# Two of four weight sums of a block pair made by accumulating DMA transfers in a Strassen-type MLP product

## The chip, the cores and the metric

The kernel runs on one core of a Trainium2 chip. The metric is the device time of one launch in microseconds. Five engines work side by side, each in the order of its own program: TensorE (PE, with its weight loads as PEld), VectorE (DVE), ScalarE (ACT), GpSimd (POOL) and SyncE (SP, here only a queue of DMA issues). They meet through semaphores alone.

## The reference

```python
def reference(x, ...):                    # x (1, 512, 2048) float32, one layer
    u = rmsnorm(h, norm_mix); z = u @ w_in
    ...                                   # RWKV-7 heads and forgetting attention, side by side
    h = h + concatenate([y_rw, y_fox]) @ w_out
    u = rmsnorm(h, norm_mlp)
    h = h + square(relu(u @ w_ff1)) @ w_ff2        # w_ff1 (2048, 8192)
    gate = sigmoid(rmsnorm(h, norm_ple) @ w_ple_gate)
    h = h + gate * (p @ w_ple_proj)
    return rmsnorm(h, norm_final)
```

The change touches `u @ w_ff1` only: 512 tokens by 2048 by 8192, in float32 accuracy.

## The kernel before, in words

Float32 accuracy is had by splitting each operand into a high part (rounded to the multiplier's format, written by ACT) and a low part (operand less high part, written by DVE) and adding three products: high by high, high by low, low by high.

For `u @ w_ff1` the kernel uses a Winograd form of Strassen's method. The weights of 256 output columns make a pair (32 pairs, `PAIRS`): b11 and b12 are the first and second 128 columns of one half of the 2048 rows (128 partitions by 8 by 128 elements, 512 KB each), b21 and b22 the same of the other half. The activations are cut in the same way into A11, A12, A21, A22 with half of the tokens each. Instead of eight block products there are seven (`UNITS`, `seven_products`, L1188): the weight operands are b11, b21, b22 and four sums, bt1 = b12 - b11, bt2 = b22 - bt1, bt3 = b22 - b12, bt4 = b21 - bt2. The activation sums S1 to S4 are made once, while the output projection before still runs (`sum_tiles`, `mix_his`, `mix_los`). Each unit is eight times a 512-column and a 256-column matmul.

How one pair flows:

- SP loads the weights in two transfers of 1 MB: part 0 holds b11 and b12, part 1 b21 and b22 (L596). Part 0 of the next pair may be loaded once bt3 is made and b11 split; part 1 once bt4 is made and b22 split (L604 to L608).
- POOL makes bt1 to bt4 by `sum_weights` (L2708), in that order. bt1 needs part 0, bt2 part 1. Each waits until the buffer's last contents have been split.
- ACT writes the high part of each unit's weights (`product_hi`, L1686), DVE the low part (`product_lo`, L2323), into four slots. A slot is free when PE has done the unit that used it, about four units back.
- PE runs the units in the order of `LATER_PAIR`: b11, b21, bt2, bt1, bt3, b22, bt4. ACT and DVE split them in another order (`LATER_TURN`), here called turns: turn 0 is bt1, turn 1 b11, turn 2 b21, turn 3 bt2, turn 4 bt3, turn 5 b22, turn 6 bt4. So the first unit of a pair (b11) can only begin when bt1 and b11 have been split.
- Between the splits DVE adds up the products out of the PSUM banks (L2347 to L2395). Its order in the loop (L2436) is: split turn 0, `take_167` and `sum_22` of the pair before, split turn 1, `sum_12`, split turn 2, `sum_21`, split turn 3, then `begin_pair` with turns 4 to 6 and the reductions between them.
- After turn 3 ACT squares the pair's hidden values and stores them to DRAM (`store_hidden`).

Pair 0 is entered while the last tile of the output projection is still being turned into activation operands; pair 1 holds the root and the reciprocal of the norm. The SBUF of `parts` and `tsum` is that of the residual h, so the first loads wait until h has been stored to DRAM tile by tile (`h_stored_again`).

Of the kernel before, what the change touches and what calls it, by code (L numbers as in the profile page):

```python
# [56 lines left out]
         "mix_split": ("narrow_split", 1), "part_landed0": ("x_landed0", 64), "part_landed1": ("x_landed1", 64),  # L57
# [54 lines left out]
def build(nc, x, p, norm_mix, w_in, mu_shift, w0, w2, a0, a2, g2, k_k, k_a, r_k, gn_w, gn_b, b_f, q_norm,  # L112
# [270 lines left out]
    staged_all = sb("staged", [P, 6, 2, T], [base + 130 * 1024])  # L383
    staged = [staged_all[:, n, :, :] for n in (0, 1, 4, 5)]
# [3 lines left out]
    b11, b12, b21, b22 = parts[:, 0, :, 0:P], parts[:, 0, :, P:], parts[:, 1, :, 0:P], parts[:, 1, :, P:]  # L388
# [25 lines left out]
    free_after = (0, 1, 1, 2, 2, 3, 3, 4)  # L414
# [11 lines left out]
    with nc.Block() as block:  # L426
# [3 lines left out]
        def _(sp):  # L430
# [163 lines left out]
            def load_part(a, cols):  # L594

                sp.dma_start(parts[:, a, :, :], ff1_parts[:, a, :, cols]).then_inc(sg(f"part_landed{a}"), 16)  # L596
# [3 lines left out]
            for a in range(2):  # L600
                load_part(a, slice(0, 2 * P))
            with sp.Fori(0, PAIRS - 1) as i:
                for a in range(2):
                    sp.wait_ge(sg("weight_sums_made"), i * 4 + (past("weight_sums_made") + a + 3))  # L604
                    sp.sem_inc(sg("waits_taken"), 1)
                    sp.wait_ge(sg("w_split"), i * UNITS + (FIRST + 4 * a + 4))
                    sp.sem_inc(sg("waits_taken"), 1)
                    load_part(a, bass.ds(i * (2 * P) + 2 * P, 2 * P))  # L608

            def load_staged(q):  # L610

                if q < 4:
                    sp.wait_ge(sg("weight_sums_made"), past("weight_sums_made") + 4 * PAIRS)
# [65 lines left out]
        def _(pe):  # L679
# [504 lines left out]
            def mixed(u, j):  # L1184

                return mix_last[:, u, :] if j == NJ else mix[:, u, j, :]

            def seven_products(i, p):  # L1188

                for u, (_, x, dst, fresh) in enumerate(pair_order(p)):  # L1190
# [11 lines left out]
                    for j in range(UK):  # L1202
                        if p == 0 and u == 0 and j in (0, NJ):
                            pe.wait_ge(sg("mix_split"), past("mix_split") + (3 * NJ if j == 0 else 3 * NJ + 1))
                        if p == 0 and u in (2, 6) and j == NJ:
                            pe.wait_ge(sg("mix_split"), past("mix_split") + 3 * NJ + (2 if u == 2 else 3))
# [75 lines left out]
        def _(act):  # L1282
# [38 lines left out]
            def root(n):  # L1321
                act.wait_ge(sg("mean_square_ready"), n + 1)
                A(tmp[:, :], tmp[:, :], ACT.Sqrt).then_inc(sg("rms_ready"), 1)
# [319 lines left out]
            def scale_tile(i, f0, b):  # L1643
# [3 lines left out]
                act.wait_ge(sg("mix_split"), i * 3 + (past("mix_split") + 3 * (f0 // 2)))  # L1647
# [9 lines left out]
            def mix_his(i, j0, which):  # L1657
# [4 lines left out]
                if which == 0:  # L1662
                    act.wait_ge(sg("tile_scaled"), i * 2 + (past("tile_scaled") + 2 * j0 + 2))
                    A(to(0, 2), ev[:, :, 0:HT], ACT.Copy).then_inc(sg("mix_hi_ready"), 1)
                if which == 1:
                    act.wait_ge(sg("sums_made"), i * 4 + (past("sums_made") + 4 * j0 + 4))
                    A(to(2, 4), tile_sums[:, :, :], ACT.Copy).then_inc(sg("mix_hi_ready"), 1)
                if which == 2:
                    if j0 != NJ:
                        act.wait_ge(sg("h_stored_again"), i * 16 + past("h_stored_again"))  # L1670
                    A(to(6, 1), ev[:, 1:2, HT:T], ACT.Copy).then_inc(sg("mix_hi_ready"), 1)

            hi_unit(1, 0, M_OUT + KT // 2, a_turn=1)
            with act.Fori(0, NJ) as i:
# [5 lines left out]
                mix_his(i, 0, 0)  # L1680
                square_tile(i, 0, 1)
                mix_his(i, 0, 1)
                mix_his(i, 0, 2)


            def product_hi(i, p, u):  # L1686

                weights = pair_order(p)[u][0]
                for n, w in enumerate((b11, b21, b22)):
                    if weights is w:  # L1690
                        act.wait_ge(sg(f"part_landed{min(n, 1)}"), i * 16 + (past(f"part_landed{min(n, 1)}") + 16 * (p + 1)))
                for n, w in enumerate((bt1, bt2, bt3, bt4)):
                    if weights is w:
                        act.wait_ge(sg("weight_sums_made"), i * 4 + (past("weight_sums_made") + 4 * p + n + 1))
# [24 lines left out]
            mix_his(0, NJ, 0)  # L1719
            product_hi(0, 0, 2)  # L1720
            square_tile(0, 2 * NJ, 1)
            mix_his(0, NJ, 1)
            mix_his(0, NJ, 2)
            for u in range(3, UNITS):
                product_hi(0, 0, u)
# [93 lines left out]
        def _(dve):  # L1819
# [43 lines left out]
            def mean_square(n, sums=bank[3], rows=1):  # L1863
                dve.wait_ge(sg("sumsq_spread"), n + 1)
                V.tensor_scalar(tmp[:, :], sums[:, :], 1.0 / (rows * D), EPS, ALU.mult, ALU.add).then_inc(sg("mean_square_ready"), 1)

            def invert_root(n):

                dve.wait_ge(sg("rms_ready"), n + 1)
                then(V.reciprocal(rstd[:, :], tmp[:, :]))  # L1870
# [431 lines left out]
            def mix_los(i, j0, which):  # L2302

                def half(u0, n, c):
                    return mix_last[:, u0:u0 + n, c] if j0 == NJ else mix[:, u0:u0 + n, bass.ds(i, 1), c].rearrange("p u a t -> p (u a) t")

                u0, n, src = ((0, 2, ev[:, :, 0:HT]), (2, 4, tile_sums[:, :, :]), (6, 1, ev[:, 1:2, HT:T]))[which]
# [459 lines left out]
```

## Time and profile before

| | us |
|---|---|
| median of three runs | 2715.71 (2709.23 to 2717.53) |
| the profiled execution, its own time | 2714.75 |
| its span (first to last instruction) | 2713.2 |
| PE busy | 2587.8 (95% of the span) |
| DVE busy | 1608.7 (59%) |
| ACT busy | 1070.8 (39%) |
| POOL busy | 593.8 (22%) |
| stage of the 32 pairs, first to last matmul | 1096.1 to 1792.3 |

A busy PE in this profile is not a PE at its peak, since the ends of pipelined matmuls are modelled. Within the pair stage DVE is busy for over 80% of the time and POOL for about half. POOL's weight sums, 64 of the form `tsum<-parts` and 64 of the form `tsum<-parts,tsum`, take 367 us together.

### The profile page before, as it was taken

What the parts mean: (1) busy time and instruction counts of PE and PEld (TensorE: products, weight loads), DVE (VectorE), ACT (ScalarE), POOL (GpSimd) and SP (SyncE); (2) the same over time, 40 slices, a digit from 0 to 9 for tenths busy, and PEclk for the clock granted to TensorE, in tenths of its full rate; (3) what the DMA queues carried; (4) which work ended last, traced back from release to release, by engine and by line L of the source; (5) the groups of instructions that cost most, each with busy time, mean ns of one, the idle gap of its engine ahead of it and who ended that gap; (6) DMA issues with size and microseconds to landing.
All of it is one profiled execution on the core that took longest, in us unless ns stands there. A gap on an engine that the chain in (4) does not pass through costs nothing.

```text
span 2713.2 us, 48534 instructions
## 1 busy us (share of the span) xinstructions
PE 2587.8 (95%) x18322; PEld 2117.5 (78%) x18322; DVE 1608.7 (59%) x2001; ACT 1070.8 (39%) x1490; POOL 593.8 (22%) x389
## 2 busy tenths in 40 slices
PE   7999999999688999799999999999999999999998
PEld 5777777777577678687878878878888888888887
DVE  5566676666545555788878888863433343444444
ACT  4443444444456325344444444442222222233333
POOL 0000000000233006555555554510000000011110
PEclk9999999999899999899999999999999999999999
DMA  7555444555523335234434343474444444333333
GB/s 200 152 153 159 144 139 143 163 162 152 184 93 101 116 101 162 86 116 131 122 118 131 116 125 118 128 235 121 120 126 120 122 117 123 93 100 106 95 97 104
DMA packets 469437, 352.26 MB, mean 130 GB/s; under 512 B 56661, under 2 KB 435527, under 8 KB 468359
## 3 DMA queue, kind: packets, MB, share of 16 engines
q1 hardware_dynamic: 413111, 281.93, 36.1%
q0 software_dynamic: 11472, 39.43, 4.2%
q10 hardware_dynamic: 44800, 30.18, 3.3%
q8 instruction: 34, 0.56, 0.1%
q14 instruction: 20, 0.16, 0.0%
HBM read 294.21 MB, written 57.28 MB: 130 GB/s over the span
## 4 chain that ended last, share of the span: by engine, by line
PE 41%; issue 33%; DVE 9%; DMA 6%; POOL 5%; ACT 5%; SPq 1%; ACTq 0%; POOLq 0%; DVEq 0%
PE acc L698 7%; PE acc L700 7%; PE acc L699 7%; PE bank L1207 5%; DMA parts<-in_w_ff 4%; DVE w_lo L2328 4%; PE bank L1208 3%; POOL tsum L2723 2%; ACT w_hi L1699 1%; ACT w_hi L1304 1%; POOL sumsq L2559 1%; PE bank L886 1%; PE acc L896 1%; PE bank L896 1%; PE bank L906 1%
## 5 line engine op out<-in xcount | busy, mean ns | idle before, releaser
L1846 DVE TENSOR_TENSOR w_lo<-w_raw,w_hi 128x1024 fp32r<-128x1024 f32 x292 | 359.7, 1232 | 682.3 <-ACT w_hi L1304 674.9
L1207 PE MATMUL bank<-mix,w_hi 128*128 128x512 f32 x1561 | 575.4, 407 | 44.8 <-DVE w_lo L2328 31.4
L1304 ACT ACTIVATE w_hi<-w_raw 128x1024 fp32r<-128x1024 f32 x292 | 308.9, 1058 | 782.9 <-PE acc L700 725.7
L1208 PE MATMUL bank<-mix,w_lo 128*128 128x256 f32 x1561 | 442.7, 284 | 0.0
L698 PE MATMUL acc<-hidden,w_hi 128*128 128x512 f32 x1024 | 399.7, 390 | 3.1 <-DVE w_lo L1846 3.1
L1207 PEld LDWEIGHTS bank<-mix,w_hi 128*128 128x128 f32 x1561 | 299.6, 192 | 128.9 <-issue 38.8
L699 PE MATMUL acc<-hidden,w_hi 128*128 128x512 f32 x1024 | 399.4, 390 | 0.0
L700 PE MATMUL acc<-hidden,w_lo 128*128 128x512 f32 x1024 | 399.3, 390 | 0.0
L698 PE MATMUL acc<-a_all,w_hi 128*128 128x512 f32 x800 | 321.1, 401 | 2.1 <-DVE w_lo L1846 2.1
L700 PE MATMUL acc<-a_all,w_lo 128*128 128x512 f32 x800 | 312.9, 391 | 0.0
L699 PE MATMUL acc<-a_all,w_hi 128*128 128x512 f32 x800 | 312.4, 390 | 0.0
L1208 PEld LDWEIGHTS bank<-mix,w_lo 128*128 128x128 f32 x1561 | 301.3, 193 | 0.2 <-issue 0.2
L2328 DVE TENSOR_TENSOR w_lo<-tsum,w_hi 128x1024 fp32r<-128x1024 f32 x128 | 208.4, 1629 | 76.6 <-ACT w_hi L1699 75.9
L698 PEld LDWEIGHTS acc<-hidden,w_hi 128*128 128x128 f32 x1024 | 192.9, 188 | 43.6 <-issue 3.5
L2723 POOL TENSOR_TENSOR tsum<-parts,tsum 128x1024 f32<-128x1024 f32 x64 | 184.2, 2878 | 186.4 <-DMA parts<-in_w_ff 135.9
L700 PEld LDWEIGHTS acc<-hidden,w_lo 128*128 128x128 f32 x1024 | 192.8, 188 | 40.2
L699 PEld LDWEIGHTS acc<-hidden,w_hi 128*128 128x128 f32 x1024 | 192.9, 188 | 40.0
L2559 POOL TENSOR_TENSOR sumsq<-sumsq,sq 128x512 f32<-128x512 f32 x31 | 43.0, 1388 | 821.0 <-ACT sq L1319 821.0
L1699 ACT ACTIVATE w_hi<-tsum 128x1024 fp32r<-128x1024 f32 x128 | 135.7, 1061 | 210.7 <-PE bank L1208 134.9
L2723 POOL TENSOR_TENSOR tsum<-parts 128x1024 f32<-128x1024 f32 x64 | 183.0, 2859 | 123.5 <-DMA parts<-in_w_ff 117.4
L698 PEld LDWEIGHTS acc<-a_all,w_hi 128*128 128x128 f32 x800 | 150.6, 188 | 56.6 <-issue 22.0
L2328 DVE TENSOR_TENSOR w_lo<-parts,w_hi 128x1024 fp32r<-128x1024 f32 x96 | 190.9, 1988 | 6.2 <-ACT w_hi L1699 6.1
(364 smaller groups left out, 3905.3 us busy)
## 6 DMA issues: line engine op xcount, KB each, us to landing
parts<-in_w_ff SPq DMA_DIRECT2D x64, 1024.0 KB, 6.0
w_raw<-in_w_ff SPq DMA_DIRECT2D x128, 512.0 KB, 3.9
w_raw<-in_w_in SPq DMA_DIRECT2D x100, 512.0 KB, 3.9
w_raw<-in_w_out SPq DMA_DIRECT2D x32, 512.0 KB, 3.9
hid_d<-sq ACTq DMA_DIRECT2D x32, 512.0 KB, 5.7
w_raw<-in_w_ple_gate SPq DMA_DIRECT2D x32, 512.0 KB, 3.9
z_d<-ev POOLq DMA_DIRECT2D x50, 256.0 KB, 3.5
ev<-hid_d SPq DMA_DIRECT2D x24, 512.0 KB, 3.5
```

Of the source, the lines that this page charges most:

```text
L698: mm(dst, wh, hi[kt], start=kt == 0, stop=False)
L699: mm(dst, wh, lo[kt], start=False, stop=False)
L700: last = mm(dst, wl, hi[kt], start=False, stop=kt == KT - 1)
L896: last = mm(low(dst[g])[o, j, :], lhs(i, g * H + j), rhs(i, g * H + j), start=lv == 1 and j == 0, stop=lv > 1 or j == H - 1, skip_group_ch ...
L1207: mm(dst[:, :], wh[:, j, :], mixed(x, j), start=fresh and j == 0, stop=False, skip_group_check=True)
L1208: last = mm(dst[:, 0:HT], wl[:, j, :], mixed(x, j)[:, 0:HT], start=False, stop=j == NJ, skip_group_check=True)
L1304: A(w_hi[:, s, :, :], w_raw[:, s ^ raw_turned[0], :, :], ACT.Copy).then_inc(sg("w_hi_ready"), 1)
L1699: A(slots[slot_of[u]][0], weights, ACT.Copy).then_inc(sg("w_hi_ready"), 1)
L1846: V.tensor_tensor(w_lo[:, s, :, 0:width], w_raw[:, s ^ raw_turned[0], :, 0:width], w_hi[:, s, :, 0:width].bitcast(F32), ALU.subtract).then ...
L2328: V.tensor_tensor(lo, weights, hi.bitcast(F32), ALU.subtract).then_inc(sg("w_split"), 1)
L2559: G.tensor_tensor(sumsq[:, :], sumsq[:, :], sq[:, b, :], ALU.add).then_inc(sg("squares_summed"), 1)
L2723: G.tensor_tensor(dst, x, y, ALU.subtract).then_inc(sg("weight_sums_made"), 1)
```

## The change

Every weight sum becomes an addition: bt1 = b11 + b12, bt3 = b12 + b22, bt2 = bt1 + b22, bt4 = bt2 + b21. The signs go into the activation sums (s1 = a21 - a22, s4 = a12 + s2) and into two adds on the product side. bt1 and bt3 are no longer made by GpSimd instructions: SP loads one block straight into the sum's buffer and POOL issues a DMA that adds the other block to it in flight (`accum_op`). So SP issues five transfers of 512 KB a pair in place of two of 1 MB, POOL two accumulating ones of 512 KB and two sums in place of four. Blocks b12 and the second use of b22 are read from DRAM, not from `parts`. `LATER_PAIR`, `LATER_TURN` and the loop order on ACT and DVE stay as they are.

```diff
-    bt1, bt2, bt3, bt4 = (tsum[:, n, :, :] for n in range(4))
-    A11, A12, S2, S1, S3, S4, A22 = range(UNITS)
-    FIRST_PAIR = ((b11, A11, bank[0], True), (b21, A12, bank[1], True), (b22, S4, bank[2], True), (bt1, S1, bank[5], True),
+    bt1, bt3, bt2, bt4 = (tsum[:, n, :, :] for n in range(4))
+    A11, A12, S1, S2, S3, S4, A22 = range(UNITS)
+    FIRST_PAIR = ((b11, A11, bank[0], True), (b21, A12, bank[1], True), (bt1, S1, bank[5], True), (b22, S4, bank[2], True),
                   (bt2, S2, bank[0], False), (bt3, S3, acc[0], True), (bt4, A22, bank[4], True))
@@ SP
-            with sp.Fori(0, PAIRS - 1) as i:
-                for a in range(2):
-                    sp.wait_ge(sg("weight_sums_made"), i * 4 + (past("weight_sums_made") + a + 3))
-                    sp.wait_ge(sg("w_split"), i * UNITS + (FIRST + 4 * a + 4))
-                    load_part(a, bass.ds(i * (2 * P) + 2 * P, 2 * P))
+            def load_parts(p, i=0):
+                def room(sums_made, turn):
+                    if p:
+                        if sums_made:
+                            sp.wait_ge(sg("weight_sums_made"), i * 2 + (past("weight_sums_made") + 2 * (p - 1) + sums_made))
+                        sp.wait_ge(sg("w_split"), i * UNITS + (FIRST + UNITS * (p - 1) + turn + 3))
+                def load(dst, a, half, landed):
+                    sp.dma_start(dst, ff1_parts[:, a, :, bass.ds(i * (2 * P) + (2 * P * p + half * P), P)]).then_inc(sg(landed), 16)
+                room(1, 2 if p == 1 else 3)
+                load(bt1, 0, 0, "u_landed")
+                room(0, 1)
+                load(b11, 0, 0, "part_landed0")
+                ...
+                room(0, 5 if p == 1 else 4)
+                load(bt3, 0, 1, "v_landed")
+                if p:
+                    room(2, 2)
+                    load(b21, 1, 0, "part_landed1")
+                    room(1, 5)
+                    load(b22, 1, 1, "part_landed2")
+            load_parts(0)
+            sp.wait_ge(sg("h_ready"), 2 * KT)
+            sp.dma_start(h_v[:, KT - 2:KT, :], h[:, KT - 2:KT, :]).then_inc(sg("last_stored"), 16)
+            load_parts(1)
+            with sp.Fori(0, PAIRS - 2) as i:
+                load_parts(2, i)
@@ ACT, pair 0
+            product_hi(0, 0, 0)
             scale_tile(0, 2 * NJ, 0)
+            mix_his(0, NJ, "A11")
             square_tile(0, 2 * NJ, 0)
-            product_hi(0, 0, 0)
             product_hi(0, 0, 1)
...
@@ DVE, pair 0
+            product_lo(0, 0, 0)
             grow_tile(0, NJ, 0)
-            product_lo(0, 0, 0)
+            mix_los(0, NJ, "A11")
...
@@ POOL
+            def add_half(i, p, name, dst, a):
+                pool.wait_ge(sg(f"{name}_landed"), i * 16 + (past(f"{name}_landed") + 16 * (p + 1)))
+                pool.sem_inc(sg("waits_taken"), 1)
+                pool.dma_start(dst, ff1_parts[:, a, :, bass.ds(i * (2 * P) + (2 * P * p + P), P)], accum_op=ALU.add).then_inc(sg(f"{name}_summed"), 16)
+            def sum_weights(i, p, last):
+                if not last:
+                    pool.wait_ge(sg("u_summed"), i * 16 + (past("u_summed") + 16 * (p + 1)))
+                    pool.wait_ge(sg("part_landed2"), i * 16 + (past("part_landed2") + 16 * (p + 1)))
+                else:
+                    pool.wait_ge(sg("part_landed1"), i * 16 + (past("part_landed1") + 16 * (p + 1)))
+                    pool.wait_ge(sg("weight_sums_made"), i * 2 + (past("weight_sums_made") + 2 * p + 1))
+                if p:
+                    pool.wait_ge(sg("w_split"), i * UNITS + (FIRST + UNITS * (p - 1) + (6 if last else 4) + 3))
...
+                dst, x, y = (bt4, bt2, b21) if last else (bt2, bt1, b22)
+                G.tensor_tensor(dst, x, y, ALU.add).then_inc(sg("weight_sums_made"), 1)
             with pool.Fori(0, PAIRS - 1) as i:
-                for n in range(4):
-                    sum_weights(i, 1, n)
+                add_u(i, 1)                # add_half of "u" into bt1
+                add_v(i, 1)                # add_half of "v" into bt3
+                sum_weights(i, 1, False)
+                sum_weights(i, 1, True)
```

`product_hi` of bt1 waits for `u_summed`, of bt3 for `v_summed`. In pair 0 the last activation tile is mixed in five steps in place of three, with b11's split ahead of the tile's work; the last store of h moves from POOL to SP; the mean square of this norm is kept in `rstd` instead of `tmp`; and the buffers of the first staged hidden tiles move by one (`free_after` of tiles 3 and 4 goes from unit 2 to unit 3).

## Rows read from the trace of the kernel before

**Rows 1.** Busy time by stretch: us long, then each engine's, PEclk, DMA share, GB/s.
```profile
1096.00:1154.00 58.00, 45.31 (x216) 37.70 (x217) 48.57 (x43) 20.93 (x23) 32.84 (x16) 0.85 0.30 91
1154.00:1773.00 619.00, 589.83 (x3261) 504.90 (x3260) 519.49 (x526) 274.14 (x262) 332.48 (x117) 0.98 0.41 123
1773.00:1793.00 20.00, 20.00 (x115) 17.32 (x114) 17.72 (x21) 13.28 (x13) 5.76 (x2) 1.00 0.73 262
1850.00:2500.00 650.00, 650.00 (x2869) 538.25 (x2868) 261.88 (x277) 166.60 (x173) 22.13 (x15) 1.00 0.39 114
```
**Rows 2.** PE's waits, 1154 to 1773 us: total us, times, longest.
```profile
PE bank L1207 <- DVE w_lo L2328: 23.5, 22, 2.9
```
**Rows 3.** Timeline of ACT, an undisturbed pair: start us, us.
```profile
1425.82 1.06 ACT L1699 ACTIVATE w_hi<-tsum 128x1024 fp32r<-128x1024 f32 x1 [1.77 <-PE bank L1208]
...
1434.30 1.06 ACT L1699 ACTIVATE w_hi<-tsum 128x1024 fp32r<-128x1024 f32 x1 [1.77 <-PE bank L1208]
```
**Rows 4.** Timeline of POOL around a PE stall.
```profile
1400.22 3.41 POOL L2723 TENSOR_TENSOR tsum<-parts 128x1024 f32<-128x1024 f32 x1 [4.02 <-DMA parts<-in_w_ff]
1406.57 2.40 POOL L2723 TENSOR_TENSOR tsum<-parts,tsum 128x1024 f32<-128x1024 f32 x1 [2.94 <-DMA parts<-in_w_ff]
1408.93 2.55 POOL L2723 TENSOR_TENSOR tsum<-parts 128x1024 f32<-128x1024 f32 x1
1411.56 3.24 POOL L2723 TENSOR_TENSOR tsum<-parts,tsum 128x1024 f32<-128x1024 f32 x1
```
**Rows 5.** Timeline of all engines around the same stall.
```profile
1403.74 1.06 ACT L1699 ACTIVATE w_hi<-tsum 128x1024 fp32r<-128x1024 f32 x1 [3.63 <-POOL tsum L2723]
...
1404.83 1.23 DVE L2328 TENSOR_TENSOR w_lo<-tsum,w_hi 128x1024 fp32r<-128x1024 f32 x1 [2.26 <-ACT w_hi L1699]
...
1406.69 2.56 DVE L2381 TENSOR_TENSOR ev<-tile_sums 128x256 f32<-128x256 f32 x1
...
1409.17 3.39 DVE L2328 TENSOR_TENSOR w_lo<-parts,w_hi 128x1024 fp32r<-128x1024 f32 x1
...
1412.49 0.41 DVE L2386 TENSOR_TENSOR ev<-bank,tile_sums 128x256 f32<-128x256 f32 x1
...
1412.69 0.49 PE L1207 MATMUL bank<-mix,w_hi 128*128 128x512 f32 x1 [2.37 <-DVE w_lo L2328]
...
1413.27 2.61 DVE L2328 TENSOR_TENSOR w_lo<-parts,w_hi 128x1024 fp32r<-128x1024 f32 x1
...
1416.59 1.22 DVE L2328 TENSOR_TENSOR w_lo<-tsum,w_hi 128x1024 fp32r<-128x1024 f32 x1
```
**Rows 6.** SP's queue in 1410 to 1414 us.
```profile
1412.81 0.38 SPq L596 DMA_DIRECT2D parts<-in_w_ff  x1
```
**Rows 7.** DMA, 1154 to 1773: queue, packets, MB, share; issues, KB, us to landing.
```profile
q1 hardware_dynamic: 60320, 60.82, 35.1%
...
parts<-in_w_ff SPq DMA_DIRECT2D x58, 1024.0 KB, 6.1
```
**Rows 8.** DMA in 1850 to 2500 us, same columns.
```profile
q1 hardware_dynamic: 127174, 73.86, 39.2%
...
w_raw<-in_w_ff SPq DMA_DIRECT2D x116, 512.0 KB, 3.9
```
**Rows 9.** DMA of the whole span, transfers issued by POOL.
```profile
h_d<-h POOLq DMA_DIRECT2D x8, 512.0 KB, 3.2
...
h<-h_d POOLq DMA_DIRECT2D x2, 2048.0 KB, 10.7
```
**Rows 10.** Line L2740: duration ns min/median/max on POOL, first and last start.
```profile
L2740 POOL DMA_DIRECT2D h<-h_d x2: 889/903/917, 1793.1 to 1821.0; - x2
```
**Rows 11.** Timeline of DVE and PE where the pair stage begins.
```profile
1092.18 3.90 DVE L2328 TENSOR_TENSOR w_lo<-parts,w_hi 128x1024 fp32r<-128x1024 f32 x1 [2.31 <-ACT w_hi L1699]
...
1096.14 0.79 PE L1207 MATMUL bank<-mix,w_hi 128*128 128x512 f32 x1 [4.54 <-DVE w_lo L2328]
...
1140.09 0.77 PE L1207 MATMUL bank<-mix,w_hi 128*128 128x512 f32 x1 [7.79 <-DVE tile_sums L2347]
```

More of the change, by code:

```diff
@@ L1184, in mixed @@
             def mixed(u, j):
+                if j == NJ and u == A11:
+                    return row_hi[:, :]
                 return mix_last[:, u, :] if j == NJ else mix[:, u, j, :]
@@ L1322, in root @@
                 act.wait_ge(sg("mean_square_ready"), n + 1)
-                A(tmp[:, :], tmp[:, :], ACT.Sqrt).then_inc(sg("rms_ready"), 1)
+                mean = rstd if n == 1 else tmp
+                A(mean[:, :], mean[:, :], ACT.Sqrt).then_inc(sg("rms_ready"), 1)
             act.wait_ge(sg("gain_transposed"), 1)
@@ L1690, in product_hi @@
                     if weights is w:
-                        act.wait_ge(sg(f"part_landed{min(n, 1)}"), i * 16 + (past(f"part_landed{min(n, 1)}") + 16 * (p + 1)))
-                for n, w in enumerate((bt1, bt2, bt3, bt4)):
+                        act.wait_ge(sg(f"part_landed{n}"), i * 16 + (past(f"part_landed{n}") + 16 * (p + 1)))
+                for summed, w in (("u_summed", bt1), ("v_summed", bt3)):
                     if weights is w:
-                        act.wait_ge(sg("weight_sums_made"), i * 4 + (past("weight_sums_made") + 4 * p + n + 1))
+                        act.wait_ge(sg(summed), i * 16 + (past(summed) + 16 * (p + 1)))
+                for n, w in enumerate((bt2, bt4)):
+                    if weights is w:
+                        act.wait_ge(sg("weight_sums_made"), i * 2 + (past("weight_sums_made") + 2 * p + n + 1))
                 freed = FIRST + 2 + UNITS * p + (u - 2 if u < 3 else u - 6 if u == 3 else u - 3)
@@ L1864, in mean_square @@
                 dve.wait_ge(sg("sumsq_spread"), n + 1)
-                V.tensor_scalar(tmp[:, :], sums[:, :], 1.0 / (rows * D), EPS, ALU.mult, ALU.add).then_inc(sg("mean_square_ready"), 1)
+                V.tensor_scalar((rstd if n == 1 else tmp)[:, :], sums[:, :], 1.0 / (rows * D), EPS, ALU.mult, ALU.add).then_inc(sg("mean_square_ready"), 1)
             def invert_root(n):
                 dve.wait_ge(sg("rms_ready"), n + 1)
-                then(V.reciprocal(rstd[:, :], tmp[:, :]))
+                then(V.reciprocal(rstd[:, :], (rstd if n == 1 else tmp)[:, :]))
             def invert_rms(n):
@@ L2317, in _ @@
                 lo_unit(1, i * 2 + (OUT_U + 3))
-                mix_los(i, 0, 0)
-                mix_los(i, 0, 1)
-                mix_los(i, 0, 2)
+                for which in ("A1", "S1", "S", "A22"):
+                    mix_los(i, 0, which)
             def product_lo(i, p, u):
@@ L2418, in _ @@
             product_lo(0, 0, 4)
-            take_fifth(0, 0, 3)
+            take_fifth(0, 0, 2)
             product_lo(0, 0, 5)
@@ L2719, in sum_weights @@
                         pool.wait_ge(sg("w_split"), FIRST + 1)
-                if n in (1, 3):
-                    pool.wait_ge(sg("weight_sums_made"), i * 4 + (past("weight_sums_made") + 4 * p + n))
-                dst, x, y = ((bt1, b12, b11), (bt2, b22, bt1), (bt3, b22, b12), (bt4, b21, bt2))[n]
-                G.tensor_tensor(dst, x, y, ALU.subtract).then_inc(sg("weight_sums_made"), 1)
-            sum_weights(0, 0, 0)
+                dst, x, y = (bt4, bt2, b21) if last else (bt2, bt1, b22)
```

128 lines of the change are left out of this document (75 added, 53 removed).

## The prediction

> **What bounds the kernel now.** I read the busy times by stretch first. In the pair stage from 1154 to 1773 us PE is busy for 589.8 of 619 us, DVE for 519.5, POOL for 332.5, and the DMA engines for a share of 0.41 [rows 1]. The stretch holds 58 weight transfers, two a pair, so 29 pairs [rows 7] at 619 / 29 = 21.3 us each. Then the timeline of ACT in an undisturbed pair: its turns are released by PE, and from turn 0 at 1425.82 to turn 3 at 1434.30 three units pass, 2.83 us a unit [rows 3]. Seven units are 19.8 us. So a pair loses 1.5 us, 44 us over 29 pairs. PE's waits say where: 23.5 us of it PE waits for DVE's low parts, 22 times, at most 2.9 us [rows 2]; some 6 more in waits for DVE's sums, and the rest is the granted clock, 0.98 of 2.4 GHz on the mean, and 0.85 where the stage begins and the stalls are longer [rows 1].
>
> The rows around one stall show why DVE is late. bt1 was made by POOL from 1400.22 to 1403.63, because part 0 landed late [rows 4]. Only then could ACT begin turn 0, at 1403.74 [rows 5]. DVE follows, but POOL runs its other three sums, and an operation of DVE with two SBUF inputs does not run beside one: 2.56 us for a sum like the one that takes 0.41, 3.39 and 2.61 us for low parts that take 1.23 [rows 5], against POOL's own 2.4 [rows 4]. PE started at 1412.69, 9.1 us after bt1 was there. PE is the bound, with small stalls; nothing else is near it over the whole stage.
>
> **What it removes.** Two of POOL's four sums, so two locks on DVE a pair, and the chain over two pairs from part 1 by bt2, bt3, part 0 to bt1. If nothing took its place, all 44 us would go. At the stage's start, b11's split moves ahead of the tile's work and no weight sum runs beside it: it took 3.90 us in place of 1.23, and PE stood for 4.54 us [rows 11]. I count -5 us there (bounds 0 and -15: the later waits of pairs 0 and 1 need bt2 and the reciprocal as before, 7.79 us the longest [rows 11], and new transfers stand before them).
>
> **What it adds: a loop from pair to pair.** SP loads bt1's buffer for the next pair after turn 3 of this pair is split. In the loop turn 3 is DVE's last split before `begin_pair`, not its first. The new chain of one pair is: U (bt1 summed) - ACT and DVE, turns 0 to 3 - SP issues the load of b11 into bt1 - it lands - POOL issues the accumulating DMA - it lands, the next U. Nothing of PE is in it, so its sum is the shortest period of a pair.
>
> 1. U to the end of turn 3. In the stalled pair it took from 1403.74 to 1417.81, 14.1 us [rows 5]. The locks in it are 2.15, 2.16 and 1.38 us, 5.7 in all; without them 8.4. Afterwards POOL makes bt2 as soon as U is there, and bt4 right behind, as b21 and b22 have landed. bt2's 2.4 us [rows 4] run while ACT splits turn 0, and hold DVE's first low part for about 1.4 us; bt4's hold the next operation for about 2. So 11.8 us (bounds 8.4 and 14.1).
> 2. SP's issue: the last low part that it needed ended at 1412.56, it issued at 1412.81 [rows 5, 6]: 0.25.
> 3. The load of 512 KB in rows of 512 B: 3.9 [rows 8].
> 4. POOL's wait, registers, and start of the issue: 0.5. The chain before shows no such step; bounds 0.1 and 0.9, the latter the whole POOL time of an issue [rows 10].
> 5. The accumulating DMA from issue to landing. No row shows one. POOL's issue itself is 0.9 us for a transfer of as many rows [rows 10]. From below: 3.2, a plain store of 512 KB by POOL [rows 9]; a plain load of the same shape by SP is 3.9 [rows 8]. From above: 10.7, POOL's 2 MB in 1024 rows [rows 9], as if adding cost four times a copy. Two things add to 3.9. It must read its destination too: one more pass of 512 KB, 39.2% of 650 us for 73.86 MB [rows 8], which is 3.45 us a MB and 1.8 for 512 KB. And it shares the engines with what SP sends in the same microseconds (the loads of bt3's half, b21 and b22, 1.8 us each); I count one of the three as ahead of it, 1.8. I take 7.5.
>
> Sum: 11.8 + 0.25 + 3.9 + 0.5 + 7.5 = 23.95 us, over PE's 19.8 and over the 21.3 of now. Twenty-nine pairs times 2.65 = +77 us. The clock's falls cost nothing more then, since PE waits anyway.
>
> A page of the Trainium skill bears on step 5. Collectives: The Full Stack, "The bandwidth ceiling", states that an add in the DMA engines costs nothing itself but needs two source reads on one ring, and so runs at half the rate of a copy. No row of this case shows an accumulating transfer. By that rule the transfer would need 3.6 us of all engines in place of 1.8, which is what I added; by a rule that an add costs as a copy does, the loop would be 1.8 us shorter, 22.15 us, and the time about 2735.
>
> **The DMA engines.** Before, q1 takes 35.1% of 619 us for 29 pairs, 7.5 us a pair; with the hidden store, by the share of 0.41, 8.8 [rows 1, 7]. After: five loads of 1.8, the store 1.3, two accumulating transfers of 1.8 to 3.6: 14 to 17.6 us in a pair. That fits in 19.8, so it is no bound alone, and 0.73 was reached for 20 us [rows 1]; but transfers will meet each other far more often, which is the reason for taking more than 5.7 in step 5. If an add cost three passes it would be 21.1, the period of today.
>
> **The rest.** POOL: two issues of 0.9 and two sums of 2.4 in place of four sums, hidden, as POOL is busy for half the stage [rows 1]. Behind its wait for `u_landed` stands the DMA for bt3, and behind that the wait for `u_summed`, with bt2 and bt4; bt3 is wanted only in turn 4, after bt2, so that costs nothing. SP: its issues are in order, b21 waits for bt4 and b22 for turn 5, and all land before U. The turned signs change no duration. The end: hidden tile 3 waits for unit 3 instead of 2, 2.8 us later, but the tiles come in after the last sum of POOL and a DMA; 0, at most +3. The norm's root in `rstd`: 0.
>
> Total: 2714.8 + 77 - 5 = 2787 us by the profiled execution's own time, 1.6 above its span; it stands 1 below the median, so 2788.
>
> **The rivals.**
> A, faster: the loop closes within PE's 19.8 us. It does if steps 1 and 5 together are at most 15.2: for instance 10 us (DVE often takes its turn ahead of POOL's second sum, and turn 0 comes early enough that only turn 3 after PE counts) and 5.2 (an add is nearly a copy). For it: step 1 without locks is 8.4, a plain transfer is 3.9. Against it: both must be near their lower bounds at once. Then the 44 us of losses shrink to a few and the start gives 5: about 2673. It decides from a loop of 21.3 on, where steps 1 and 5 are 16.6.
> B, no change: the loop is 21.1 to 21.8 us, either by an add at the cost of a copy without crowding or by step 1 near 9.5. 2715.
> C, far slower: adding in flight costs more than two passes, or crowding takes three loads, so that step 5 is 10.7 or more. The loop is then 27.2 and more: 29 x 5.9 = +171, about 2880. Against it: nothing shows the engines near their limit now.
>
> **How the numbers follow.** Forecast 0.60, A 0.24, B 0.08, C 0.08. The forecast's own range, with step 1 from 11.5 to 12 and step 5 from 5.7 to 9.5, a loop of 21.9 to 26.2: 2730 to 2850. The range for 8 in 10 takes in most of A: 2668 to 2850. A measurement of this kernel tells 0.3%, 8 us, from no change. Faster 0.24; same 0.08; slower 0.68.
>
> **What would show it.** Right: PE waits for w_lo in almost every pair, 3 to 4 us each, at the first unit; the starts of the `hid_d` stores are 23 to 25 us apart; ACT's turn 0 is released by the DMA into tsum, not by PE; turn 3's low part, SP's load and POOL's issue follow each other without slack; the accumulating DMA lands 7 to 8 us after its issue. DVE's low parts have a lower mean than now, without PE gaining. Wrong: ACT's turn 0 still released by PE, or pairs 19.8 to 20.5 us apart (A), or the accumulating DMA landing within 5 us. At the start, b11's low part near 1.2 us and PE waiting under 1 us for it.

## The result, and the profile after

The changed kernel takes 2889.94 us (median of four runs, 2886.96 to 2890.87) against 2716.62 for the kernel before beside it: a ratio of 1.0643, with a 95% interval of 1.0624 to 1.0663. The forecast was 2788, with a range up to 2850. The sign and the mechanism were right, and the size was 2.4 times the forecast's: the profiled span grew from 2713.2 to 2888.7 us, by 175.5 where 72 had been summed. In this section and in the experiments two readings do most of the work: the distance of the `hid_d` stores, of which there is one a pair, so that their distance is the period of a pair, and the chain of waits through one pair.

First the busy times by stretch of the changed kernel, in the columns of [rows 1]:

```profile
1096.00:1154.00 58.00, 42.00 (x210) 35.10 (x210) 41.81 (x41) 22.04 (x26) 28.60 (x17) 0.88 0.80 164
1154.00:1900.00 746.00, 598.66 (x3062) 514.98 (x3063) 470.74 (x498) 255.50 (x247) 234.32 (x109) 0.87 0.71 153
```

PE was busy for 95% of the pair stage before and is busy for 80% of it now. Every engine is busy for a smaller share of it; only the DMA engines' share has risen, from 0.41 to 0.71. A stage in which no engine is the bound is bound by a chain of waits. The stores give its period; ahead of them the same row of the kernel before (duration min/median/max in ns, first and last start in us):

```profile
L1712 ACTq DMA_DIRECT2D hid_d<-sq x32: 338/338/353, 1134.4 to 1799.8; - x32
```

```profile
L1751 ACTq DMA_DIRECT2D hid_d<-sq x32: 338/338/353, 1131.4 to 1974.3; - x32
```

There are 31 steps between 32 stores. Before, a step was 665.4 / 31 = 21.46 us; after, 842.9 / 31 = 27.19. 31 x 5.73 = 177.5 us, less 3.0 because the first store comes earlier, plus 1.0 behind the last one: 175.5, the whole difference of the spans.

The waits of the changed kernel between 1200 and 1900 us (total us, times, longest), which answer to [rows 2]:

```profile
POOL tsum L2761 <- DMA tsum<-in_w_ff: 343.0, 50, 11.2
...
ACT w_hi L1738 <- DMA tsum<-in_w_ff: 162.4, 22, 8.1
...
PE bank L1234 <- DVE w_lo L2373: 138.3, 26, 6.1
```

PE waits for a low part once in each of the 26 pairs of this stretch, 5.3 us on the mean, where it was 22 short waits in the whole stage before. Behind it stands ACT's turn 0, which waits for the accumulating DMA into bt1. The chain of waits shows the loop itself. Here is one period, from the low part of turn 3 in one pair to that of the next (start us, us, what), with its small pieces left out:

```profile
1486.03 1.23 DVE w_lo L2373
...
1487.48 4.56 DMA tsum<-in_w_ff
...
1492.99 9.34 DMA tsum<-in_w_ff
...
1502.43 1.07 ACT w_hi L1738
...
1509.22 1.21 DVE w_lo L2373
...
1511.14 1.22 DVE w_lo L2373
...
1513.06 1.22 DVE w_lo L2373
...
1514.52 4.76 DMA tsum<-in_w_ff
...
1520.13 9.61 DMA tsum<-in_w_ff
...
1529.76 0.04 ACTq L1737
```

All five steps of the prediction's loop can be read off. Turn 3's low part ends at 1487.26; SP issues the load of b11 into bt1 at 1487.48; it lands 4.56 us later; POOL's issue of the accumulating DMA starts at 1492.99; it lands after 9.34 us; ACT begins turn 0 at 1502.43, and turn 3's low part ends at 1514.28, 27.02 us after the last one. There is no matmul in the chain.

What SP and POOL sent around that accumulating transfer, from the timelines of SP and then of POOL:

```profile
1514.52 0.37 SPq L606 DMA_DIRECT2D tsum<-in_w_ff  x1
1515.13 0.39 SPq L606 DMA_DIRECT2D parts<-in_w_ff  x1
1518.63 0.37 SPq L606 DMA_DIRECT2D tsum<-in_w_ff  x1
1519.47 2.82 SPq L606 DMA_DIRECT2D parts<-in_w_ff  x2
```

```profile
1520.13 1.56 POOL L2761 DMA_DIRECT2D tsum<-in_w_ff  x1 [11.12 <-DMA tsum<-in_w_ff]
1524.86 1.55 POOL L2761 DMA_DIRECT2D tsum<-in_w_ff  x1 [3.17 <-DMA tsum<-in_w_ff]
```

Three loads (bt3's half, b21, b22) leave within 3.7 us, around the accumulating DMA's issue at 1520.13; the load of b11, issued at 1515.13 and landed 7.0 us later, still runs for its first 2 us. bt3's own accumulating DMA follows at 1524.86; after it neither queue sends anything until the next turn 3. The DMA view of 1200 to 1900 us, in the columns of [rows 7]:

```profile
q1 hardware_dynamic: 132623, 66.87, 36.2%
q0 software_dynamic: 53719, 27.08, 30.7%
...
parts<-in_w_ff SPq DMA_DIRECT2D x76, 512.0 KB, 6.9
tsum<-in_w_ff SPq DMA_DIRECT2D x52, 512.0 KB, 5.0
tsum<-in_w_ff POOLq DMA_DIRECT2D x51, 512.0 KB, 9.0
```

q0 holds the 51 accumulating transfers: 0.307 x 700 / 51 = 4.2 us of all 16 engines each. q1 holds the 128 loads: 0.362 x 700 / 128 = 2.0 us each.

The median of 9.0 us mixes two kinds of transfer. Taken one by one between 1160 and 1950 us, the accumulating DMAs into bt1 land in 9.6 us (median of 29, 9.1 to 10.2) and those into bt3 in 8.5 (8.2 to 9.2). Only the first kind stands in the chain above, and it is the one compared in the experiments.

At the start of the stage, where [rows 11] had PE's first product of the pairs at 1096.14 after a wait of 4.54 us, the timelines of DVE and of PE now say:

```profile
1088.99 3.72 DVE L2373 TENSOR_TENSOR w_lo<-parts,w_hi 128x1024 fp32r<-128x1024 f32 x1
```

```profile
1092.77 0.50 PE L1234 MATMUL bank<-mix,w_hi 128*128 128x512 f32 x1 [1.08 <-DVE w_lo L2373]
```

b11's low part is still slow (3.72 us; POOL's sum of squares of the last tile runs beside it from 1089.65 to 1091.61), but it begins 3.2 us earlier, and the first product comes 3.4 us earlier.

### The profile page after: what moved, and what is told of

Same layout as the page of the kernel before. It is cut to its first block, busy times and chain, and to the rows that moved or that the text cites. A ratio compares the mean times of both kernels' runs of the same rounds, so it can differ in the third digit from the quotient of the medians.

```text
span 2888.7 us, 49206 instructions
## 1 busy us (share of the span) xinstructions
PE 2633.7 (91%) x18322; PEld 2158.6 (75%) x18322; DVE 1584.7 (55%) x2010; ACT 1067.8 (37%) x1499; POOL 502.6 (17%) x388
## 4 chain that ended last, share of the span: by engine, by line
PE 37%; issue 31%; DMA 16%; DVE 10%; ACT 4%; POOL 1%; SPq 1%; DVEq 0%; POOLq 0%; ACTq 0%
DMA tsum<-in_w_ff 14%; PE acc L723 7%; PE acc L725 7%; PE acc L724 7%; DVE w_lo L2373 4%; PE acc L1130 2%; PE acc L1132 2%; PE acc L1131 2%; PE bank L1234 1%; ACT w_hi L1738 1%; ACT w_hi L1331 1%; POOL sumsq L2606 1%; PE bank L911 1%; PE bank L921 1%; DVE tile_sums L2421 1%
## 5 line engine op out<-in xcount | busy, mean ns | idle before, releaser
L1234 PE MATMUL bank<-mix,w_hi 128*128 128x512 f32 x1561 | 618.4, 430 | 174.8 <-DVE w_lo L2373 166.8
L1234 PEld LDWEIGHTS bank<-mix,w_hi 128*128 128x128 f32 x1561 | 322.8, 207 | 263.0 <-issue 176.9
L1235 PE MATMUL bank<-mix,w_lo 128*128 128x256 f32 x1561 | 463.7, 297 | 0.0
L2373 DVE TENSOR_TENSOR w_lo<-tsum,w_hi 128x1024 fp32r<-128x1024 f32 x128 | 214.7, 1678 | 218.0 <-ACT w_hi L1738 218.0
L1235 PEld LDWEIGHTS bank<-mix,w_lo 128*128 128x128 f32 x1561 | 325.2, 208 | 0.2 <-issue 0.2
L2784 POOL TENSOR_TENSOR tsum<-tsum,parts 128x1024 f32<-128x1024 f32 x64 | 176.1, 2752 | 137.8 <-DMA parts<-in_w_ff 132.8
L2761 POOL DMA_DIRECT2D tsum<-in_w_ff x64 | 99.9, 1561 | 431.4 <-DMA tsum<-in_w_ff 417.5
L725 PEld LDWEIGHTS acc<-a_all,w_lo 128*128 128x128 f32 x800 | 150.5, 188 | 32.3
```

Of the source, the lines that this page charges most:

```text
L725: last = mm(dst, wl, hi[kt], start=False, stop=kt == KT - 1)
L1234: mm(dst[:, :], wh[:, j, :], mixed(x, j), start=fresh and j == 0, stop=False, skip_group_check=True)
L1235: last = mm(dst[:, 0:HT], wl[:, j, :], mixed(x, j)[:, 0:HT], start=False, stop=j == NJ, skip_group_check=True)
L2373: V.tensor_tensor(lo, weights, hi.bitcast(F32), ALU.subtract).then_inc(sg("w_split"), 1)
L2761: pool.dma_start(dst, ff1_parts[:, a, :, bass.ds(i * (2 * P) + (2 * P * p + P), P)], accum_op=ALU.add).then_inc(sg(f"{name}_summed"), 16)
L2784: G.tensor_tensor(dst, x, y, ALU.add).then_inc(sg("weight_sums_made"), 1)
```

## The experiments

Kernels are named by their labels. Those with an interval were timed in several rounds; the others are one run each. The kernel before stood beside them at 2709.46 (median) for e1 to e3 and e6, 2709.04 (one run) for e4, e5, e8 and e10, 2713.6 for e6b, e7 and e11, and 2716.35 for e12. The period is always (last store - first store) / 31 of the `hid_d` stores.

**e1_early_load: is it a loop, or the DMA engines?** The one wait that closes the loop is SP's, before it loads bt1's buffer. The buffer is free when turn 0 is split and bt2 is made; the changed kernel waits for turn 3.

```diff
-            def load_parts(p, i=0):
+            def load_parts(p, i=0, first=3):
-                room(1, 2 if p == 1 else 3)
+                room(1, 2 if p == 1 else first)
                 load(bt1, 0, 0, "u_landed")
-            with sp.Fori(0, PAIRS - 2) as i:
-                load_parts(2, i)
+            load_parts(2)
+            with sp.Fori(0, PAIRS - 3) as i:
+                load_parts(3, i, first=0)
```

> Changed kernel with one edit: from the fourth pair on SP may load bt1's buffer for the next pair once turn 0 (bt1) is split and bt2 is made, not only after turn 3. Theory 1, the loop from pair to pair (bt1 summed, turns 0 to 3, SP's load, POOL's accumulating DMA) sets the time: now 11.9 + 0.25 + 5.6 + 9.65 = 27.3 us; turn 0 ends 4.4 us after bt1 is summed, so the loop is 4.4 + 0.25 + 5.6 + 9.65 = 19.9 us, PE's own 19.8 is reached in places: 20 to 21 us a pair, total 2700 to 2725 us. Theory 2, the DMA engines are the bound (busy 0.71 of 27.1 us, 19.3 us a pair): the transfers crowd each other and land later the closer the pairs come, the period stays at 22 us or more, total 2750 us or more.

Measured: 2692.86 us (2689.41 to 2697.42), a ratio of 0.9937 (0.9919 to 0.9956) to the kernel before. One wait was worth 1.0643 - 0.9937 of the time before, 192 us, and what had lost 6.4% gains 0.6%. The time is 7 us under theory 1's range, with the period of 20.87 us inside the 20 to 21 that it gave, and far from theory 2's. Busy times and DMA view of 1200 to 1750 us in e1:

```profile
1200.00:1750.00 550.00, 535.30 (x3005) 460.40 (x3004) 441.18 (x484) 251.40 (x242) 230.56 (x108) 0.99 0.97 205
```

```profile
q0 software_dynamic: 55512, 27.99, 42.2%
...
parts<-in_w_ff SPq DMA_DIRECT2D x80, 512.0 KB, 7.8
tsum<-in_w_ff POOLq DMA_DIRECT2D x54, 512.0 KB, 7.0
```

The loop theory holds. The DMA engines are at a share of 0.97 here, and PE is busy for 97% of the stretch all the same. The accumulating transfers into bt1 land in 7.5 us (median; 6.8 to 9.4), sooner than the 9.6 of the changed kernel with its engines at 0.72, while SP's loads into `parts` land later than there (7.8 against 6.9). Within e1 the landing goes by what is issued next to it: 6.8 us where the next load of SP leaves 2.1 us behind the transfer, 9.4 where it leaves 0.8 us behind. So the mean load does not explain the 9.6; that the transfers of the same few microseconds do is what these readings and e3 below point to.

**e2_plain_copy: what does the adding cost?** The accumulating DMAs become plain ones.

```diff
-    ... (2 * P * p + P), P)], accum_op=ALU.add).then_inc(...)
+    ... (2 * P * p + P), P)]).then_inc(...)
```

> Changed kernel with the two DMAs of POOL as plain copies: the additions of bt1 and bt3 are left out. What the addition itself costs. If the second read is the cost (64.7 ns a packet against 30.9 for a plain one), POOL's transfer lands in 5.5 to 7 us in place of 9, the period is about 24 us and the total 2790 to 2810. If POOL's own way of issuing and the crowding by SP's loads are the cost, it still lands after 8.5 us or more, and the total stays above 2860.

Measured: 2830.58 us. Period 25.47 us, 1.7 less than in the changed kernel. Its DMA view of 1200 to 1750 us:

```profile
q0 software_dynamic: 6080, 22.15, 14.1%
...
tsum<-in_w_ff POOLq DMA_DIRECT2D x44, 512.0 KB, 6.9
```

Taken one by one, the plain copies land in 7.6 us into bt1 and 6.3 into bt3 (medians), where the accumulating ones took 9.6 and 8.5: in the same crowd the adding costs 2.0 to 2.2 us of landing, in which stands whatever its smaller packets cost (see the last section). By the periods the time fell by 31 x 1.72 = 53 us; it lies between the two expectations, nearer to the first. The adding is under a third of the loss of 178 us, not the whole of it.

**e3_thin and e4_thin_plain: the same without the crowd.** From pair 1 on every transfer of weights but the two into bt1 moves one eighth of its rows (bt3's DMA from POOL too, in the same way), so most of the weights stay those of pair 0; e4 also has plain copies, and leaves the two additions out as e2 does.

```diff
-    sp.dma_start(dst, ff1_parts[:, a, :, ...]).then_inc(sg(landed), 16)
+    n = 1 if p and landed != "u_landed" else UK
+    sp.dma_start(dst[:, 0:n, :], ff1_parts[:, a, 0:n, ...]).then_inc(sg(landed), 16)
```

> Changed kernel in which, from pair 1 on, all loads but that into bt1, and the accumulating DMA into bt3, move one eighth of their rows (most of b11, b21, b22, b12 stay those of pair 0). The accumulating DMA into bt1 has the engines to itself. If crowding took 3 us of its 9.65 (as at the start of the stage, where one landed after 6.7 us), it lands after 6.5 to 7 us, the load after 4.5, the period is 23.3 us and the total about 2780. If its time is its own, it still lands after 9 us or more, and the total is above 2850.

> As the thin kernel (all loads but that into bt1 cut to one eighth from pair 1 on), and POOL's two DMAs are plain copies, so the additions are left out. The transfer into bt1 alone, copy against accumulation, with the engines to itself. If the second read costs about 2 us, it lands after 4.7 to 5 us where the accumulating one took 6.9, the period is 21.3 us in place of 23.1, and the total 2720 to 2730 in place of 2773. If an add costs nothing, it lands after 6.5 us or more and the total stays at 2765 or more.

Measured: 2773.07 us for e3 (period 23.60) and 2722.13 for e4 (period 22.01). The transfers that POOL sends into bt1, from the DMA view of 1200 to 1750 us of e3 and then of e4:

```profile
tsum<-in_w_ff POOLq DMA_DIRECT2D x24, 512.0 KB, 6.9
```

```profile
tsum<-in_w_ff POOLq DMA_DIRECT2D x25, 512.0 KB, 5.0
```

Without company the accumulating transfer lands in 6.9 us and the plain one in 5.0. So the 9.6 us of the transfer into bt1 are 5.0 for the copy as POOL sends it, 1.9 for the adding, and 2.6 for the company (9.56 - 6.92). The other way round, by e2, the company costs a plain copy 2.5 us (7.57 - 5.02) and the adding in that company 2.0: the two ways agree. e3 came within 7 us of what the loop theory had expected and e4 within its range, though e4's period was expected at 21.3.

**e5_u_by_pool and e8_both_by_pool: GpSimd in place of the DMA, the loop left closed.** SP loads b12 into bt1's buffer and GpSimd adds b11 from `parts`, in place; e8 does the same for bt3 with b22. The load still waits for turn 3.

```diff
-                add_half(i, p, "u", bt1, 0)
+                pool.wait_ge(sg("u_landed"), ...)
+                pool.wait_ge(sg("part_landed0"), ...)
+                G.tensor_tensor(bt1, bt1, b11, ALU.add).then_inc(sg("u_summed"), 16)
```

> Changed kernel with one part undone: bt1 is made by GpSimd in place (b12 loaded, b11 added), bt3 still by the accumulating DMA; the load still waits for turn 3. Loop theory: 11.9 + 0.25 + 6.1 (two loads) + 2.9 (the sum) = 21.1 us in place of 27.3, total 2700 to 2730. If what costs is any accumulating DMA beside the loads, wherever it stands, half of the loss stays: 2790 or more.

> Changed kernel with no accumulating DMA at all: bt1 and bt3 by GpSimd in place, four GpSimd sums a pair as before the change; signs, five loads of 512 KB, the new start and the late load stay. Loop theory: again 21.1 us plus what a fourth GpSimd sum holds VectorE up in the loop (0 to 1.5 us), total 2705 to 2745. If the accumulating DMA of bt3 costs as such, this is faster than the kernel with bt1 alone undone by more than 10 us.

Measured: 2762.19 us for e5 (period 23.23) and 2805.83 for e8 (24.48). Both missed their ranges, by 32 and 61 us, and e8 is slower than e5 by 44, where the two ranges had overlapped. The timelines of POOL and of SP in e5:

```profile
1484.56 2.96 POOL L2766 TENSOR_TENSOR tsum<-tsum,parts 128x1024 f32<-128x1024 f32 x1 [13.01 <-DMA parts<-in_w_ff]
```

```profile
1476.72 0.37 SPq L606 DMA_DIRECT2D tsum<-in_w_ff  x1
1477.43 0.37 SPq L606 DMA_DIRECT2D parts<-in_w_ff  x1
```

The sum does not wait for bt1's buffer but for b11, which SP sends behind it: 7.84 us from SP's first issue, where some 6 had been expected; then 2.96 for the sum. With 12.05 for the turns and 0.25 for the issue this is the period, 23.1. It is still a loop, four microseconds shorter than with the accumulating DMA. e8 shows something new. POOL works in order, so bt3's sum, which needs b22, the last load of a pair, now stands ahead of bt2's, and turn 3 waits for bt2: 80.7 us in 23 waits of ACT. The expectation had allowed up to 1.5 us a pair for a fourth sum holding DVE up, and nothing for its place in the queue. The lock is seen too: in the pair at 1470 us two low parts take 3.40 and 2.63 us, where e5's has 3.42 and 1.22 at the same place.

**e6_u_by_pool_early (and again as e6b): both ideas together.** bt1 by GpSimd in place as in e5, bt3 by the accumulating DMA, the early load as in e1.

> Changed kernel with bt1 made by GpSimd again, in place (b12 is loaded into bt1's buffer, b11 added there), bt3 still by the accumulating DMA, and the early load of the first experiment. Loop theory: 4.4 + 0.25 + 6.6 (two loads) + 0.2 + 3 = 14.5 us, under PE's 19.8; only bt3's accumulating DMA is left, with 10 us to spare. So PE is the bound: 20 to 20.4 us a pair, total 2665 to 2690, faster than both kernels. Theory 2 (DMA engines, now about 15 us a pair): also no bound. If locks between GpSimd and VectorE are what is left, the pair stays near 21.3 us and the total near 2710.

> The kernel of e6_u_by_pool_early again, on another chip job, beside the two below: 2670 to 2680 us, 0.985 to 0.990 of the kernel before by every theory. It gives the line against which the next two are read.

Measured: 2674.5 us (2671.62 to 2675.56), a ratio of 0.987 (0.9854 to 0.9887), and in the second job 2674.8, 0.9871 (0.9849 to 0.9892). This beats both kernels: the one before by 1.3% in either job (35 us by the ratios), the changed one by 0.077 of the time before, 210 us. Period 20.30 us; PE is busy for 540.9 of the 550 us from 1200 on, and ACT is released by PE, as in an undisturbed pair of before [rows 3]:

```profile
ACT w_hi L1739 <- PE bank L1236: 239.3, 150, 1.8
```

**e10_v_by_pool and e11_v_by_pool_early: the mirror of e5 and e6.** bt1 by the accumulating DMA, bt3 by GpSimd in place; e10 with the late load, e11 with the early one.

```diff
-                add_half(i, p, "v", bt3, 1)
+                pool.wait_ge(sg("v_landed"), ...)
+                pool.wait_ge(sg("part_landed2"), ...)
+                G.tensor_tensor(bt3, bt3, b22, ALU.add).then_inc(sg("v_summed"), 16)
```

> Changed kernel with the other part undone: bt3 is made by GpSimd in place (b12 loaded, b22 added), bt1 still by the accumulating DMA; the load still waits for turn 3. Loop theory: the accumulating DMA of the loop stays, less crowded (it lands after 8 to 9 us in place of 9.65), the period is 25.5 to 26.5 us, total 2830 to 2865. If cost goes by the number of accumulating DMAs, this comes out as the kernel with only bt1 undone does.

> bt1 by the accumulating transfer, bt3 by GpSimd in place, load of bt1's buffer released after turn 0: it asks whether the order on POOL (bt3's sum waits for b22 and stands ahead of bt2's) is what made e10_v_by_pool slower than the changed kernel. Theory 1 (e10 lost by turn 3 coming late in the loop, so with the load taken off turn 3 it no longer matters): 2690 to 2715 us, close to e1_early_load's 2693. Theory 2 (a GpSimd sum of bt3 is slow in itself, by its lock on DVE in turns 3 and 4): 2740 or more.

Measured: 2956.79 us for e10 (period 29.26), slower than the changed kernel with one accumulating DMA fewer; and for e11 2799.68 us (2793.03 to 2802.25), ratio 1.0332 (1.031 to 1.0353).

e10 missed its range of 2830 to 2865 us by 92. From its DMA view of 1200 to 1750 us:

```profile
tsum<-in_w_ff POOLq DMA_DIRECT2D x19, 512.0 KB, 9.5
```

The accumulating DMA into bt1 was expected after 8 to 9 us and lands after 9.5, as in the changed kernel, though bt3's is gone: its company is SP's loads, not the other accumulating DMA. The loop is the old one with a longer step 1: turn 3 waits for bt2 behind bt3, and turn 0 to turn 3's low part takes from 1476.15 to 1490.01, 13.9 us in place of 11.85. In e11 turn 3 is out of that loop, and theory 1 expected 2690 to 2715. It fell. The number is within theory 2's, but its reason, that a GpSimd sum of bt3 is slow in itself by its lock on DVE, does not fit e7 below, which has that sum and bt1's as well and is level with the kernel before. The chain of waits of e11 shows a second loop, which neither theory had (small pieces left out):

```profile
1446.74 2.60 DVE w_lo L2374
...
1450.24 1.07 ACT sq L1748
1451.34 1.07 ACT sq L1750
...
1453.03 1.07 ACT w_hi L1739
...
1456.06 1.23 DVE w_lo L2374
...
1457.52 7.07 DMA parts<-in_w_ff
...
1464.73 0.07 POOL tsum L2770
...
1467.10 3.38 POOL tsum L2787
```

Turn 5 (b22) is split by 1457.29; only then may b22 be loaded, which takes 7.07 us; POOL makes bt3 out of it, then bt2, until 1470.48; turn 3 needs bt2, and turn 5 stands behind turn 3 on ACT and DVE, with the squares between. Turn 3 began at 1445.06 and begins again at 1470.58: 25.5 us for this pair, 24.15 on the mean. Without bt3's sum this loop is shorter by 2.4 us. The low part at 1446.74, 2.60 us in place of 1.22, stands beside bt4's sum (1445.11 to 1448.26), which the changed kernel has too. What tells e11 from e7 is the landing of b22, taken one by one: 7.6 us on the median against 4.3, with periods of 24.15 and 21.12. That the accumulating DMAs beside it make b22 late, and b22 the pair, fits both traces; no run isolates it.

**e7_both_by_pool_early and e12_both_by_pool_bt2_first: does the accumulating DMA earn anything?** No accumulating transfer at all, early load; e12 only swaps two sums on GpSimd.

```diff
                 add_u(i, 1)
-                add_v(i, 1)
                 sum_weights(i, 1, False)
+                add_v(i, 1)
                 sum_weights(i, 1, True)
```

> No accumulating transfer at all: bt1 and bt3 both made by GpSimd in place (bt1 += b11, bt3 += b22), with the load of bt1's buffer released after turn 0. It asks whether the one accumulating transfer left in e6_u_by_pool_early earns anything once the loop is open. Theory 1 (the second lock counts): a fourth GpSimd sum of 3 us a pair holds DVE's low parts as in the kernel before, and bt3's sum stands ahead of bt2's in POOL's queue, waiting for b22: 2690 to 2710 us. Theory 2 (with the loop open PE has slack enough for four sums, and only the late load was the trouble): 2670 to 2680, as e6_u_by_pool_early. POOL's wait for b22 ahead of bt3's sum should be seen in both; what differs is whether PE waits for w_lo behind it.

> e7_both_by_pool_early with one swap in GpSimd's loop: bt2's sum before bt3's. Still no accumulating transfer. It asks what the accumulating transfer of bt3 earned in e6_u_by_pool_early (2674 against 2713 us). Theory 1 (the place in the queue: bt3's sum between b22's landing and bt2's sum lengthens a second loop, turn 5 split - b22 loads - bt3 - bt2 - turn 3 to 5, by its 2.4 to 3.4 us): bt2 comes at once again, and the time falls to 2675 to 2690 us. Theory 2 (the lock: a fourth sum on GpSimd holds DVE's low parts, wherever it stands): 2700 to 2715, as before the swap. In between, 2690 to 2700, would mean both.

Measured: e7 2713.39 us (2704.94 to 2717.34), ratio 0.9999 (0.9983 to 1.0014), within 4 us of theory 1's upper end and 33 over theory 2's; e12 2688.62 us (2683.67 to 2692.76), ratio 0.9894 (0.9874 to 0.9915). ACT's longest waits in e7, and then in e12:

```profile
ACT w_hi L1739 <- PE bank L1236: 201.0, 131, 2.0
...
ACT w_hi L1739 <- POOL tsum L2789: 80.2, 27, 3.0
```

```profile
ACT w_hi L1739 <- PE bank L1236: 245.7, 162, 1.9
```

With the swap no wait of ACT for a sum of POOL is left, and the time falls by 1.05% by the ratios, into theory 1's range; between the two profiled executions it is 18 us, with periods of 21.12 and 20.65. Of the 1.28% between e6b and e7, measured side by side, 1.05 was then the place of bt3's sum in GpSimd's queue. What is left for the lock of a fourth sum is the distance of e12 to e6b: 0.9894 against 0.9871 by the ratios, 6 us, with intervals that overlap. By the plain medians it is 14 us (2688.62 against 2674.8), in different jobs whose kernels before lie 3 us apart, and the profiled periods are 20.65 and 20.30. So once the sum stands in the right place, the accumulating DMA in its stead earns some 0.2 to 0.4%; by the ratios that is not told from nothing.

## Why the prediction was right and wrong, step by step

The bound before and the loop. Right: PE was the bound before; it is not now. The new chain of one pair is the one that was written down, step for step, with no matmul in it, so that PE's granted clock of 0.87 in place of 0.98 costs nothing more. The marks that were named for it are there: a release of turn 0 by the DMA into tsum, a wait of PE for w_lo in every pair, hardly any slack between turn 3, SP's load and POOL's issue. Their sizes were not as named: PE's wait is 5.3 us and not 3 to 4, the stores are 27.19 us apart and not 23 to 25, and the accumulating DMA lands after 9.6 and not 7 to 8. The mean of the low parts made from `parts` fell, from 1997 to 1243 ns; that of the ones made from `tsum` rose, from 1585 to 1681. PE gained nothing by it. e1 shows the loop by cutting it: 192 us with one wait.

Step 1, the turns: forecast 11.8, measured 11.85. The two locks of POOL's sums that it was built from are there as well: 3.29 us for a low part that takes 1.22, and 1.85 for a sum that takes 0.41, 3.5 in all where 1.4 + 2 had been taken. From DVE's timeline of the same pair:

```profile
1503.53 3.29 DVE L2373 TENSOR_TENSOR w_lo<-tsum,w_hi 128x1024 fp32r<-128x1024 f32 x1 [5.25 <-ACT w_hi L1738]
...
1507.45 1.85 DVE L2426 TENSOR_TENSOR ev<-tile_sums 128x256 f32<-128x256 f32 x1
```

Step 2, SP's issue: forecast 0.25, measured 0.22 and 0.24.

Step 3, the load of b11: forecast 3.9, measured 4.6 to 4.8 in the chain, 5.0 as a median. The row used [rows 8] is from a later stage with the engines at 0.39, without company. Alone in e3 the load takes 4.5.

Step 4, POOL's wait and registers: forecast 0.5 (bounds 0.1 and 0.9), measured 0.95 and 0.85.

Step 5, the accumulating DMA: forecast 7.5, measured 9.3 and 9.6 in the chain, 9.6 as a median. This is the step that failed, the term of the sum that was mis-sized most. It had been summed as 3.9 for a copy, 1.8 for the second read and 1.8 for one load ahead. Measured they are 5.0 (e4), 1.9 (e3 less e4) and 2.6 (the changed kernel less e3). The adding was right to a tenth of a microsecond, its smaller packets counted in. The copy was too cheap by 1.1: the nearest row for a plain transfer into bt1 was one of SP's queue, and POOL's stores of [rows 9] write in the other direction. The crowd was too light by 0.8: three loads are issued beside it and b11's is still under way, where one was counted as ahead.

The Trainium skill, Collectives: The Full Stack, "The bandwidth ceiling", says of the reduce step of a collective that the add in the DMA engines itself is free, while its two source reads halve the rate. The trace agrees for these transfers: 4.2 us of all engines for an accumulating one of 512 KB, against 2.0 for a load of SP in the same stretch and in packets of the same size; and 0.141 x 550 / 44 = 1.8 for a plain one from POOL's queue in e2.

The sum. The loop was forecast at 23.95 us and is 27.19: 0.8 of the difference is from step 3, 0.4 from step 4, 2.0 from step 5. Over 31 periods that is 100 us, and the miss is 102 (2890 against 2788); that 29 pairs were counted where there are 31 periods, and 21.3 us for a period of before that is 21.46, cancel each other to a microsecond by luck. The range's upper end had step 5 at 9.5 but held steps 3 and 4 fixed, and so ended at 26.2 a pair. Rival C had nearly the time (2880) and a loop of 27.2, by a step 5 of 10.7 that was not reached; three loads of crowding, one of its two reasons, is near what was found. Rival B's first case was summed wrongly: an add at the cost of a copy without crowding makes step 5 3.9 us and the loop 20.35, not 21.1 to 21.8.

The DMA engines: forecast 14 to 17.6 us a pair, measured 0.715 x 27.19 = 19.4 (the sum of the queues' shares, 36.2, 30.7 and 4.6%), since an accumulating transfer takes 4.2 and a load 2.0 where 1.8 was taken. They were not the bound, as said. In e1 they nearly are, at 0.97 of a period of 20.87 us, and ACT still waits there for the DMA into tsum in most pairs; e6, with one accumulating DMA a pair and a share of 0.77, has a period of 20.30. "14 to 17.6" had made them look far from PE's 19.8, and they were not.

The start: forecast -5 (bounds 0 and -15), measured -3.0 by the first store. PE's wait there is 1.08 us, as forecast in size. It was not b11's low part that became fast (3.72 us; the forecast had it near 1.2, with only the weight sum gone from beside it, but POOL's work for the last tile is still there), but its begin that came earlier.

POOL's queue: "that costs nothing" was right for the changed kernel, where bt3 is made by a DMA and its wait ends before bt2's. e7 and e12 price the same place in the queue at 28 us by the ratios (18 between the profiled executions) as soon as a sum that needs b22 stands in it.

What stays open is how the 44 us from e5 to e8, and the 4% from e1 to e11, divide between the place of bt3's sum, its lock on DVE and the crowding. Only for e7 was the order swapped. That the company of bt1's accumulating DMA is SP's loads follows from e3 and e10 together; which of them, and how much their timing does, no run shows, since none moves them alone. Nor does a run split e1's distance to e6 (0.9937 against 0.987) into the load of the DMA engines and the longer way of bt1.

## What to carry to other kernels

When a transfer takes over an instruction, write down the chain of one iteration to the next: who frees the buffer, who loads it, who adds. If that chain has no instruction of the bounding engine in it, its sum is the period, and landings in it must be priced as they are in a crowd of their own stage (4.7 and 9.6 us here, not 3.9 and 7.5).

Free a buffer at its last reader. Here the load waited for turn 3, and its last readers were turn 0 and one sum; that one wait decided between 6.4% slower and 0.6% faster, more than the choice of engine did.

On an engine that works in order, a sum with a late operand goes behind the one that others wait for: up to 1% here for swapping two lines.

## What was not expected of the hardware

An accumulating DMA of 512 KB, in rows of 512 B, took 1.56 us of POOL for its issue, where a plain one of the same shape took 0.9 (e2), and 4.2 us of the sixteen engines where the plain copy of e2 took 1.8.

The packets differ too: the 44 plain copies of e2 are 6080 packets for 22.15 MB, about 3.6 KB each, while the accumulating ones keep to 504 B (53719 for 27.08 MB), as SP's loads do (504 B). SP's plain loads in packets of 504 B take 2.0 us of the engines, close to the 1.8 of e2's large packets, so the packets' size does not seem to make the 4.2; for the landing of POOL's transfers these runs do not separate the size from the second read.

With the DMA engines at a share of 0.97 (e1) the accumulating DMA into bt1 landed in 7.5 us on the median, near the 6.9 of e3 with the engines at 0.39, though SP's loads into `parts` came later than in the changed kernel. At 0.72, with SP's loads issued within 2 us of it, it took 9.6.
